# Two model blocks in one kernel on one core: a third unscaled group behind each norm of the first block, finer loads, waits and sums, 128 bytes of padding, and a convolution in another place

## The reference

```python
def hybrid_layer(x, ...):
    h = rms_norm(x, norm_w)                 # x * rsqrt(mean(x*x) + eps) * w
    p = h @ w_in
    ... = jnp.split(p, splits, axis=-1)     # idx_q, idx_k, ckv, q, z, sb_*, ml_*, merge
    y_a = dsa_attention(...)
    y_b = stick_breaking_attention(...)
    ml_q, ml_k = jnp.split(jax.nn.silu(causal_depthwise_conv(ml_qk, conv_w)), 2, axis=-1)
    h_c = mlstm_chunkwise(...)
    ...
    mixed = jnp.sum(gates * proj, axis=2)
    return x + mixed @ w_out
```

## Time and profile before

| | |
|---|---|
| median of three runs | 2614.61 us (2613.52 to 2619.84) |
| the profiled execution: its time | 2612.44 us |
| its span in the trace | 2610.7 us, 31966 instructions |
| PE busy (matmuls) | 2532.7 us, 97% |
| DVE, ACT, POOL busy | 1097.9, 1063.0, 1308.6 us (42, 41, 50%) |
| granted clock of PE over the span | 0.993 |
| moved by DMA | 227.21 MB, a mean of 87 GB/s |

### The profile page before, as it was taken

How to read it: one execution, slowest core, us unless ns; L and a number is a source line. 1 busy time by engine, 2 the same in 40 slices (tenths; PEclk the granted TensorE clock), 3 DMA queues, 4 the chain that set the end, 5 groups by cost and what they waited for, 6 DMA issues and landing times.

```text
span 2610.7 us, 31966 instructions
## 1 busy us (share of the span) xinstructions
PE 2532.7 (97%) x12502; PEld 2037.2 (78%) x12502; DVE 1097.9 (42%) x1891; ACT 1063.0 (41%) x1604; POOL 1308.6 (50%) x1790
## 2 busy tenths in 40 slices
PE   7999999999999999999999999999989899999998
PEld 5778787788777878768878888878867688888886
DVE  4864544622476554462242213088445422311101
ACT  4434566423443456642343323242355333422321
POOL 4444464455545446545555555485433255555453
PEclk9999999999999999999999999999999999999999
DMA  3232112123222212222232232242221132222322
GB/s 143 82 101 79 59 57 89 66 97 97 97 73 81 74 57 65 81 73 97 94 108 94 97 98 92 90 153 65 83 71 65 43 97 97 96 97 97 97 97 81
DMA packets 63409, 227.21 MB, mean 87 GB/s; under 512 B 7399, under 2 KB 8935, under 8 KB 62876
## 3 DMA queue, kind: packets, MB, share of 16 engines
q1 hardware_dynamic: 60988, 217.28, 25.1%
q0 software_dynamic: 2272, 7.90, 1.1%
HBM read 222.98 MB, written 4.01 MB: 87 GB/s over the span
## 4 chain that ended last, share of the span: by engine, by line
PE 88%; DVE 5%; ACT 4%; POOL 1%; issue 1%; DMA 0%; SPq 0%; DVEq 0%; ACTq 0%
PE proj L166 75%; PE att L890 1%; PE proj L853 1%; PE proj L960 1%; DVE hT L511 1%; POOL weight_low L144 1%; DVE h_low L505 1%; ACT b_logits L2350 1%; PE att L166 1%; PE att L832 1%; PE att L876 1%; PE att L843 1%; PE att L934 1%; DVE rstd L1469 1%; PE proj L737 0%
## 5 line engine op out<-in xcount | busy, mean ns | idle before, releaser
L144 POOL TENSOR_TENSOR weight_low<-ring,weight_high 128x256 fp32r<-128x256 f32 x1592 | 1234.1, 806 | 1151.2 <-ACT weight_high L125 1127.8
L166 PE MATMUL proj<-h_high,weight_high 128*128 128x512 f32 x2032 | 805.8, 397 | 19.7 <-ACT b_big L2193 13.0
L166 PE MATMUL proj<-h_high,weight_low 128*128 128x512 f32 x2032 | 794.5, 391 | 0.0
L166 PE MATMUL proj<-h_low,weight_high 128*128 128x512 f32 x2032 | 794.2, 391 | 0.0
L125 ACT ACTIVATE weight_high<-ring 128x1024 fp32r<-128x1024 f32 x393 | 414.1, 1054 | 415.4 <-PE proj L166 380.4
L166 PEld LDWEIGHTS proj<-h_high,weight_high 128*128 128x128 f32 x2032 | 382.6, 188 | 135.4 <-ACT b_big L2193 14.3
L166 PEld LDWEIGHTS proj<-h_low,weight_high 128*128 128x128 f32 x2032 | 382.8, 188 | 80.8
L166 PEld LDWEIGHTS proj<-h_high,weight_low 128*128 128x128 f32 x2032 | 383.1, 189 | 76.5 <-issue 0.2
L2541 DVE TENSOR_TENSOR b_big<-proj,b_big 128x512 f32<-128x512 f32 x42 | 29.0, 691 | 376.3 <-PE proj L166 376.3
L166 PE MATMUL proj<-b_act_high,weight_high 128*128 128x512 f32 x352 | 137.6, 391 | 0.4 <-POOL weight_low L144 0.4
L166 PE MATMUL proj<-b_act_low,weight_high 128*128 128x512 f32 x352 | 137.2, 390 | 0.0
(11 more groups left out here) (469 smaller groups left out, 3719.5 us busy)
## 6 DMA issues: line engine op xcount, KB each, us to landing
ring<-in_stream SPq DMA_DIRECT2D x398, 512.0 KB, 3.3
idx<-gate_rows POOLq DMA_DIRECT2D x16, 256.0 KB, 4.3
xT<-in_x SPq DMA_DIRECT2D x2, 1024.0 KB, 6.6
out<-hT SPq DMA_DIRECT2D x4, 512.0 KB, 2.7
bias_rows<-bias_row SPq DMA_DIRECT2D x2, 512.0 KB
b_logits<-in_mem POOLq DMA_DIRECT2D x1, 1024.0 KB, 6.0
consts<-in_const SPq DMA_DIRECT2D x1, 832.0 KB, 10.5
bias_rows<-bias_row SPq DMA_DIRECT2D x1, 768.0 KB
```

Of the source, the lines that this page charges most:

```text
L144: self.s_low.on(pool.tensor_tensor(self.low[:, c % self.slots, cols], self.raw[:, c % self.slots, cols], self.high[:, c % HIGH, cols], ALU ...
L166: mm = pe.matmul(out, a, b, start=(k == 0 and i == 0), stop=(k == n - 1 and i == 2))
```

## The change

- **Third group.** `idx2` is an OWN lead group in both layers (bank `att[2]`), scaled by DVE like the other two; the first group that waits for h is `misc`. In layer 0 the group `ms` stands behind `idx0`: the total is taken at step 3 of `idx1` and the spread at step 5 (elsewhere the total at step 6 of the first lead group and the spread at the beginning of the second, as before).
- **Finer parts.** x is loaded in four parts, each with its own semaphore; `const2` comes behind chunk 1, and PE waits for it only ahead of the total. Chunk 0 is rounded in four pieces (`round_first`) after the second scaled copy, and chunk 1 after the second square. PE waits for the pieces of a chunk that the step needs and not for the whole chunk.
- **Sums.** The running sum of squares and the first square (except ffn1's) lie in PSUM (`att[4]`); the last addition goes to `rstd`.
- **Padding.** 32 floats a partition (128 bytes) are allocated behind `vecs`, so that all the first block's tiles from `dq` on move by 128 bytes.
- **Convolution.** conv(4) comes behind the second `soft_rest` of pair 0.

```diff
@@ -41,8 +41,10 @@
 BANKS = [(0, 512, 0), (1, 512, 512), (2, 256, 1024)]
 
+LINE_UP = 32
+X_PARTS = 4
@@ -134,12 +136,23 @@
+    def round_first(self, act):
+
+        act.wait_ge(self.s_load[0].sem, 16)
+        for i in range(PIECES):
+            cols = slice(i * UNIT // PIECES, (i + 1) * UNIT // PIECES)
+            self.s_high.on(act.activation(self.high[:, 0, cols], self.raw[:, 0, cols], ACT.Copy))
+        self.n_high = 1
+
     def rest(self, pool, result):
 
         while self.due(self.n_low, HIGH, result):
             c = self.n_low
-            pool.wait_ge(self.s_high.sem, c + 1)
             for i in range(PIECES):
+                if c == 0:
+                    pool.wait_ge(self.s_high.sem, i + 1)
+                elif i == 0:
+                    pool.wait_ge(self.s_high.sem, c + PIECES)
                 cols = slice(i * UNIT // PIECES, (i + 1) * UNIT // PIECES)
                 self.s_low.on(pool.tensor_tensor(self.low[:, c % self.slots, cols], self.raw[:, c % self.slots, cols],
                                                  self.high[:, c % HIGH, cols], ALU.subtract))
@@ -149,9 +162,10 @@
 
         pos, n, width = self.place[self.tile_of[self.G.part + result]]
         c, off = divmod(pos + k * width, UNIT)
-        if c >= self.n_seen:
-            pe.wait_ge(self.s_low.sem, PIECES * (c + 1))
-            self.n_seen = c + 1
+        pieces = PIECES * c + -(-(off + width) * PIECES // UNIT)
+        if pieces > self.n_seen:
+            pe.wait_ge(self.s_low.sem, pieces)
+            self.n_seen = pieces
         return self.high[:, c % HIGH, off:off + width], self.low[:, c % self.slots, off:off + width]
 
     def product(self, pe, result, out, xs, tokens=False, ready=None):
@@ -221,7 +235,8 @@
 def layer_groups(l):
 
     toep = lambda i: [(f"toep{i}", "a")] if l == 0 else []
-    g = [("ms", "a"), ("idx0", OWN), ("idx1", OWN), ("idx2", "a"), ("misc", "a"), ("ridx0", "v"), ("idx3", "a"),
+    g = [("idx0", OWN), ("ms", "a"), ("idx1", OWN)] if l == 0 else [("ms", "a"), ("idx0", OWN), ("idx1", OWN)]
+    g += [("idx2", OWN), ("misc", "a"), ("ridx0", "v"), ("idx3", "a"),
          ("ridx1", "v"), ("q0", "a"), ("ridx2", "v"), ("iwt", "a"), ("q1", "a"), ("cms", "a"), ("q2", "a")]
     g += toep(0) + [("q3", "a")] + toep(1) + [("rkr", "a")]
     for i in range(4):
@@ -401,6 +416,11 @@
 LEADS = ["0", "1", "ffn1", "ffn2"]
 
 
+def square_place(S, n, k):
+
+    return S.att[4][:, :] if k == 0 and n != "ffn1" else S.hT[:, k, :]
+
+
 def norm_squares(S, act, n, ready, lead=None):
 
     act.preload_act_table_set("sqrt_and_others")
@@ -409,7 +429,7 @@
         if lead is not None:
             high, _, weights = lead
             S.s_lh.on(act.activation(high[:, k, :], S.xT[:, k, :], ACT.Copy, scale=weights[:, k:k + 1]))
-        S.s_sq.on(act.activation(S.hT[:, k, :], S.xT[:, k, :], ACT.Square))
+        S.s_sq.on(act.activation(square_place(S, n, k), S.xT[:, k, :], ACT.Square))
 
 
 def norm_copy(S, act, n):
@@ -430,12 +450,16 @@
 
     high, low, _ = lead
 
+    total, spread = ((1, 3), (1, 5)) if n == NORMS[0] else ((0, KD - 2), (1, 0))
+
     def ready(k):
         if i == 0:
             pe.wait_ge(S.s_ll.sem, KD * LEADS.index(n) + k + 1)
-            if k == KD - 2:
-                norm_total(S, pe, n, name)
-        elif k == 0:
+        if (i, k) == total:
+            if n == NORMS[0]:
+                pe.wait_ge(S.s_in_first.sem, 16)
+            norm_total(S, pe, n, name)
+        if (i, k) == spread:
             norm_spread(S, pe, n)
     S.W.product(pe, result, S.att[i][:, :], [(high[:, k, :], low[:, k, :]) for k in range(KD)], ready=ready)
 
@@ -443,18 +467,19 @@
 def norm_sum(S, dve, n, k):
 
     at = KD * NORMS.index(n)
-    rstd, hT = S.rstd, S.hT
+    total, hT = S.att[4][:, :], S.hT
+    out = total if k < KD - 1 else S.rstd[:]
     dve.wait_ge(S.s_sq.sem, at + k + 1)
     if n == "ffn1":
         w = S.pair_sq[:, k:k + 1]
         if k == 0:
-            ins = dve.tensor_scalar(rstd[:], hT[:, 0, :], w, None, ALU.mult)
+            ins = dve.tensor_scalar(out, hT[:, 0, :], w, None, ALU.mult)
         else:
-            ins = dve.scalar_tensor_tensor(rstd[:], hT[:, k, :], w, rstd[:], ALU.mult, ALU.add)
+            ins = dve.scalar_tensor_tensor(out, hT[:, k, :], w, total, ALU.mult, ALU.add)
     else:
         if k == 0:
             return
-        ins = dve.tensor_tensor(rstd[:], hT[:, 0, :] if k == 1 else rstd[:], hT[:, k, :], ALU.add)
+        ins = dve.tensor_tensor(out, total, hT[:, k, :], ALU.add)
@@ -545,6 +570,7 @@
     s_a, s_v, s_ac, s_vc = S.s_a, S.s_v, S.s_ac, S.s_vc
 
     both_vecs = sb("vecs", [P, DEPTH, N_VEC])
+    sb("line_up", [P, LINE_UP])
     dq_at, dq = here(nc), sb("dq", [P, 4, T])
@@ -689,13 +715,13 @@
         act.preload_act_table_set("sqrt_and_others")
         high, _, weights = lead_of(0)
         for k in range(KD):
-            act.wait_ge(S.s_x[k // 4].sem, 16)
+            act.wait_ge(S.s_x[k * X_PARTS // KD].sem, 16)
             S.s_lh.on(act.activation(high[:, k, :], xT[:, k, :], ACT.Copy, scale=weights[:, k:k + 1]))
-            if k == 3:
-                W.round_one(act)
+            if k == 1:
+                W.round_first(act)
         for k in range(KD):
-            S.s_sq.on(act.activation(hT[:, k, :], xT[:, k, :], ACT.Square))
-            if k == 3:
+            S.s_sq.on(act.activation(square_place(S, NORMS[0], k), xT[:, k, :], ACT.Square))
+            if k == 1:
                 W.round_one(act)
         act.wait_ge(S.s_set.sem, 3)
 
@@ -718,7 +744,7 @@
         def dense(name):
 
             out = G.open(pe, name)
-            ready = (lambda k: pe.wait_ge(S.s_hl.sem, KD * l + k + 1)) if name == "idx2" else None
+            ready = (lambda k: pe.wait_ge(S.s_hl.sem, KD * l + k + 1)) if name == "misc" else None
             W.product(pe, name, out[:, :], h_parts, ready=ready)
 
         def dense_tokens(n, i):
@@ -744,11 +770,9 @@
                 s_sc.on(pe.matmul(bank[:, col:col + WQ[b]], idx[r, h // 2, b * P:(b + 1) * P], idx[r, 2, 0:WQ[b]],
                                   start=True, stop=True))
 
-        if l == 0:
-            pe.wait_ge(S.s_in_first.sem, 16)
         lead_product(S, pe, NORMS[l], "idx0", 0, lead_of(l), "ms")
         lead_product(S, pe, NORMS[l], "idx1", 1, lead_of(l), "ms")
-        dense("idx2")
+        lead_product(S, pe, NORMS[l], "idx2", 2, lead_of(l), "ms")
         dense("misc")
         if l == 0:
             pe.wait_ge(S.s_in_consts.sem, 16)
@@ -756,7 +780,7 @@
         dense("idx3")
         rotated("ridx1", idx[:, 1, :], 1)
         dense("q0")
-        rotated("ridx2", idx[:, 2, :], "idx2")
+        rotated("ridx2", idx[:, 2, :], 2)
         out = G.open(pe, "iwt")
         G.moved(pe, "misc")
         for b in range(TB):
@@ -1011,7 +1035,6 @@
                 s_relu.on(act.activation(relu[:, n % 4, 0:WQ[b]], bank[:, col:col + WQ[b]], ACT.Relu))
 
         norm_copy(S, act, NORMS[l])
-        move("idx2", idx[:, 2, :])
         move("misc", misc[:])
         settle(act, s_a)
         s_ir.on(act.activation(g_i, misc[32:32 + ML_H, :], ACT.Identity, bias=vecs[32:32 + ML_H, 45:46]))
@@ -1254,7 +1277,7 @@
                 norm_sum(S, dve, NORMS[0], k)
         norm_scale(S, dve, NORMS[l], "ms", hT, vecs[:, 0:KD])
         dve.wait_ge(S.s_copied.sem, l + 1)
-        for i in range(2):
+        for i in range(3):
             G.whole(dve, f"idx{i}")
             s_led.on(dve.tensor_tensor(idx[:, i, :], att[i][:, :], rstd[:], ALU.mult))
         if l == 0:
@@ -1419,10 +1442,8 @@
             soft_sum(p, 0)
             soft_sum(p, 1)
             soft_rest(p, 0)
-            if p == 0:
-                conv(4)
             soft_rest(p, 1)
-            for h in ([5, 6], [7], [], [])[p]:
+            for h in ([4, 5, 6], [7], [], [])[p]:
                 conv(h)
             for i in ([], range(4), [], range(4, 8))[p]:
                 centre(i)
@@ -3117,15 +3138,16 @@
 
             @block.sync
             def _(sp):
-                half = KD // 2
+                n = KD // X_PARTS
                 S.s_in_vecs.on(sp.dma_start(one["both_vecs"][:], A["vec"]), 16)
-                S.s_x[0].on(sp.dma_start(S.xT[:, 0:half, :], A["x"][:, 0:half, :]), 16)
-                S.W.load(sp, 0, A["stream"][0])
-                S.s_x[1].on(sp.dma_start(S.xT[:, half:KD, :], A["x"][:, half:KD, :]), 16)
-                S.s_in_first.on(sp.dma_start(S.consts[:], A["const2"]), 16)
+                for i in range(X_PARTS):
+                    S.s_x[i].on(sp.dma_start(S.xT[:, n * i:n * i + n, :], A["x"][:, n * i:n * i + n, :]), 16)
+                    if i == 0:
+                        S.W.load(sp, 0, A["stream"][0])
                 for c in range(1, S.W.n_chunks):
                     S.W.load(sp, c, A["stream"][c])
                     if c == 1:
+                        S.s_in_first.on(sp.dma_start(S.consts[:], A["const2"]), 16)
                         S.s_in_consts.on(sp.dma_start(one["consts"][:], A["const"]), 16)
```

(4 more changed lines are left out.)

## The result

The changed kernel takes 2595.92 us (median of 4 runs, 2594.42 to 2600.33), against 2617.07 for the kernel before in the same session: ratio 0.9924, 95% interval 0.9911 to 0.9936. It is faster by 0.76%, where 0.82% and 2593.2 us were predicted. Its profiled execution has a span of 2593.4 us, 17.3 less than before, where the sum said 21.4.

The account below looks back on a forecast made before the run. TensorE (PE), busy 97% of the span, was taken to bound the kernel. Terms 8.0 + 1.5 + 5.8 + 6.1 = 21.4 us took the median of 2614.61 to 2593.2; 8-in-10 range 2587 to 2602.

Parts of the forecast that it names:

- The start: Layer 0 up to misc: PE starts near 8 us, additions take 0.70; 8.0 us won, bounds 4.9 and 9.0.
- the open question: Layer 0's start: whether PE's 1.9 us wait for the sum brings half clock, losing 1.7 us again.
- Third group of layer 1: Layer 1, idx2: three waits for normalized tiles and their resumes go; 1.5 us won, bounds 0.7 and 1.6.
- Convolution: Pair 0 of stick-breaking, two layers: moving conv(4) removes long wait and half clock; 5.8 us, or 2.7 if half clock stays.
- Its two rivals: Pair 0: half clock stays, or POOL stays slow as conv is one of two neighbours; 2596 to 2599, chance 0.06.
- Padding: Matmuls over mix, z and lead get faster on the 512-byte grid; 6.1 us won, bounds 7.1 and -3.4.
- The loss on the stick-breaking sums: Stick-breaking sums: probs, turned and bias go off the grid; 160 matmuls by 6.5 ns, 1.0 us lost.
- The rule set against it: Padding: the skill says PE never waits on anyone, so padding is worth nothing and the time 6.1 us longer.
- tiles on or off a grid of 512 bytes: Padded tiles: an operand off a multiple of 512 bytes runs PE 3% slower, 233.3 against 226.5 ns.
- x in four parts: Rival at the start: two more loads cost 4 us if fixed cost is serial; time 2597, chance 0.04.
- The sum: Whole kernel: 8.0 + 1.5 + 5.8 + 6.1 = 21.4 us won.
- The step that failed: Search for PE's waits: of PE rows with idle time ahead, only those the diff touches were examined, three places.

Follow-up runs that it names:

- sums_in_sbuf: The changed kernel with the running sum of squares back in rstd and square 0 back in hT, both SBUF: 2600.2 us.
- lags_apart: The changed kernel with second-block steps LAGS and IN(1) asked one filler product later and GpSimd's three 512 KB loads spread by weight_low rounds: 2593.08 us.
- conv_back: The changed kernel with conv(4) back between the two halves of soft_rest of pair 0: 2602.47 us.
- no_padding: The changed kernel without its 128 bytes of padding: 2603.71 us.
- all_moved_384: The changed kernel with 384 bytes of padding ahead of its first tile, so every operand moves alike: 2594.55 us.
- x_two: The changed kernel with x in two loads, as before, and all else of the start as changed: 2599.97 us.

## Why the prediction was right, and what it missed

- *The start*: 8.0 predicted in the middle, 8.8 at full clock; 8.63 measured. Additions at 0.70 us: each took 0.70, 0.74 from start to start, and sums_in_sbuf shows that PSUM is why (up to 1.12 without). PE's wait was 1.27 us and not 1.9: PE started at 8.68 and not at 8, and the wait for the sum took that up, so the error cost nothing. It may even have been luck, since the open question was whether the half clock would come: there was none behind 1.27 us, and none behind 1.67 in lags_apart, half behind 2.67. What 1.9 us would have brought here no run shows.
- *Third group of layer 1*: 1.5 predicted, 1.8 measured, a little above its bounds.
- *Convolution*: 5.8 predicted, 2.9 and 2.9 measured. Its two rivals fell with conv_back.
- *Padding*: 6.1 predicted, 6.1 measured, but by terms both too large. Summing the distances of starts by kind of operand in no_padding and the changed kernel, z gave 2.7 us, mix 2.6 and lead 0.8, against 7.1 in all. The z matmuls had lost some 5 ns each and not 6.3. The loss on the stick-breaking sums, 1.0 predicted, was 0.1 (137.0 against 137.6 ns for 160 matmuls). By the declared shapes that fits the distance: their weights, `signs`, lie in `misc`, which moves by the same 128 bytes as probs and bias, so no distance within these sums changed. The rule set against it, that PE never waits on anyone (the Trainium skill, "SBUF — State Buffer", Who interferes with whom), would make the padding worth nothing, and these rows do not bear that out: nothing but addresses differs between no_padding and the changed kernel, and all_moved_384 rules out the place by itself. The prediction's reading, tiles on or off a grid of 512 bytes, was too narrow: 256 bytes off was as fast, and it is the distance to the weights that counts.
- *x in four parts*: not dear, as the prediction had it. The last part landed 0.6 to 1.3 us later than in x_two, mostly under ACT's work; a gain is not shown.
- *The sum*: 21.4 predicted; the parts as measured one by one, 8.6 + 1.8 + 5.8 + 6.1, make 22.3, and the lead in front of LAGS is 22.3. That these agree is partly luck. Most of the padding's 0.8 us on lead operands is counted in the start and the third group as well, 1.4 us were lost to half clock in layer 1, and 1.8 came from a term that the prediction put at nothing without a reason: the finer waits for POOL's pieces outside the start (2.7 us with the one at 1885). No run takes these out, so that term rests on the vanished waits alone.
- *The step that failed* stands in the first paragraph: "looked only at those that the diff touches", among rows with idle time ahead of them. LAGS had none and 0.1 us of slack. A PE that comes 22 us earlier is harmless only if the engine that feeds it comes as much earlier, and DVE came 16.9. The wait and the clock behind it took 7.2 us, of which finer waits and half clocks elsewhere gave back 3.7; the predicted 2593.2 became 2595.9, inside the range. So the time came out right with every priced mechanism confirmed, but the closeness of the sum owes something to terms that were not in it.

## What to carry to other kernels

Where a change brings the bound engine forward, list also the places where it does not wait yet but its feeder has less slack than the change brings, and give them slack in the same change (here: ask one product later, 3 to 6 us). A matmul's moving operand should stand at the same place within 256 bytes as its weights: it is free to arrange and was worth 2 to 3% of the affected products (0 and 256 bytes apart were fast, 384 slow, 128 not tried). Compare traces instruction by instruction, as a lead: that separates parts of 2 us, which the times, with half clocks that fall differently in each execution, cannot. And look for a change to a shared helper wherever the helper is used: the finer waits were priced at the start only.

## What was unexpected of the hardware

- A matmul's pace went with the distance of its two SBUF operands: 226.5 ns at 0 and 256 bytes apart within 512, 233.3 at 384; 128 was not tried.
- Behind one and the same wait of 3.42 us the granted clock was 1.00 in one execution and 0.68 in another; behind waits of 1.79 and 1.81 us at pair 0 it was 0.61 in all four places in two kernels, behind 0.44 and 1.27 us it was 1.00.
- An addition of 128x512 on DVE beside POOL's subtractions took 1.02 to 1.12 us with both operands in SBUF and 0.70 with one in PSUM, and POOL's pieces took up to 1.19 us beside the first and 0.74 beside the second.
- A chunk of 512 KB that lands in 3.3 us alone took 6.5 to 8.7 us when issued among three other loads of its size, and 4.7 with those spread over 8 us.
